# Round 0 of a top-k search reads its bank, a reversal moves to ScalarE, gates are made last, the first expert tile starts with rounded rows

## The reference

```python
probs = jax.nn.softmax(jnp.einsum('bld,de->ble', h, w_router), axis=-1)
scores = jnp.transpose(probs, (0, 2, 1))            # 16 experts x 1024 tokens
gate, idx = lax.top_k(scores, cap)                  # cap = 128
xs = jax.vmap(lambda hb, ib: hb[ib])(h, idx)
a = jnp.einsum('becd,edf->becf', xs, w_gate)        # 1024 -> 2048
u = jnp.einsum('becd,edf->becf', xs, w_up)
y = jnp.einsum('becf,efd->becd', jax.nn.silu(a) * u, w_down)
y = (y * gate[..., None]).astype(h.dtype)
out = jax.ops.segment_sum(y.reshape(-1, dm), seg, num_segments=bn * seq)
```

## Time and profile before

| | us |
|---|---|
| median of 3 runs | 2847.98 (2847.28 to 2848.88) |
| profiled execution | 2847.89 |
| its span | 2846.1 |

### The profile page before, as it was taken

How to read it: one execution, slowest core, us unless ns; L and a number is a source line. 1 busy time by engine, 2 the same in 40 slices (tenths; PEclk the granted TensorE clock), 3 DMA queues, 4 the chain that set the end, 5 groups by cost and what they waited for, 6 DMA issues and landing times.

```text
span 2846.1 us, 33534 instructions
## 1 busy us (share of the span) xinstructions
PE 2790.2 (98%) x13774; PEld 2342.7 (82%) x13774; DVE 1836.6 (65%) x2051; ACT 1514.2 (53%) x1618; POOL 136.5 (5%) x81
## 2 busy tenths in 40 slices
PE   8999999879999999999999999999999999999999
PEld 7889988768888888888888877888888888888887
DVE  8563467778888888888888895332332356544344
ACT  5322322247777777777777775333333389733022
POOL 0211000110000000000000000000000011100000
PEclk9999999989999999999999999999999999999999
DMA  6222157789999999999999951110212211243332
GB/s 200 89 77 75 71 177 263 274 310 377 388 383 390 381 389 382 381 391 382 390 384 388 380 200 74 60 53 31 60 60 60 69 48 63 95 159 132 111 133 89
DMA packets 137273, 598.97 MB, mean 210 GB/s; under 512 B 17952, under 2 KB 39840, under 8 KB 80672
## 3 DMA queue, kind: packets, MB, share of 16 engines
q1 hardware_dynamic: 132224, 580.10, 54.5%
q0 software_dynamic: 4464, 16.25, 2.2%
q10 hardware_dynamic: 432, 0.47, 0.1%
HBM read 543.06 MB, written 52.53 MB: 209 GB/s over the span
## 4 chain that ended last, share of the span: by engine, by line
PE 95%; DVE 3%; ACT 1%; issue 0%; DMA 0%; SPq 0%; DVEq 0%; ACTq 0%
PE bank L442 25%; PE bank L444 25%; PE bank L443 25%; PE bank L1835 12%; PE bank L450 3%; PE bank L2391 1%; PE bank L1406 1%; PE bank L778 1%; PE bank L2763 0%; DVE r_sc L1628 0%; DVE r_at L1629 0%; DVE r_best L1625 0%; PE bank L2392 0%; DVE b_x L2189 0%; PE bank L838 0%
## 5 line engine op out<-in xcount | busy, mean ns | idle before, releaser
L1794 DVE TENSOR_TENSOR e_wl<-e_raw,e_wh 128x2048 fp32r<-128x2048 f32 x381 | 870.8, 2292 | 126.4 <-ACT e_wh L1786 125.6
L1786 ACT ACTIVATE e_wh<-e_raw 128x2048 fp32r<-128x2048 f32 x384 | 735.8, 1919 | 187.0 <-PE bank L444 106.5
L442 PE MATMUL bank<-b_hid_h,b_wh 128*128 128x512 f32 x1152 | 454.0, 394 | 3.1 <-DVE t_v L2619 1.1
L444 PE MATMUL bank<-b_hid_h,b_wl 128*128 128x512 f32 x1152 | 449.0, 390 | 0.0
L443 PE MATMUL bank<-b_hid_l,b_wh 128*128 128x512 f32 x1152 | 448.5, 389 | 0.0
L442 PE MATMUL bank<-e_wh,e_xh 128*128 128x512 f32 x1024 | 405.7, 396 | 1.7 <-DVE e_xl L1934 1.7
L444 PE MATMUL bank<-e_wh,e_xl 128*128 128x512 f32 x1024 | 400.2, 391 | 0.0
L443 PE MATMUL bank<-e_wl,e_xh 128*128 128x512 f32 x1024 | 398.9, 390 | 0.0
L442 PEld LDWEIGHTS bank<-b_hid_h,b_wh 128*128 128x128 f32 x1152 | 216.4, 188 | 50.4 <-issue 5.4
L444 PEld LDWEIGHTS bank<-b_hid_h,b_wl 128*128 128x128 f32 x1152 | 216.2, 188 | 45.8
L443 PEld LDWEIGHTS bank<-b_hid_l,b_wh 128*128 128x128 f32 x1152 | 216.5, 188 | 42.8
(11 more groups left out here) (490 smaller groups left out, 4337.3 us busy)
## 6 DMA issues: line engine op xcount, KB each, us to landing
e_raw<-in_e_gate_dram SPq DMA_DIRECT2D x128, 1024.0 KB, 7.2
e_raw<-in_e_up_dram SPq DMA_DIRECT2D x128, 1024.0 KB, 7.7
e_raw<-in_e_down_dram SPq DMA_DIRECT2D x128, 1024.0 KB, 7.6
b_raw<-in_w_dram SPq DMA_DIRECT2D x36, 1024.0 KB, 5.8
a_raw<-in_w_dram SPq DMA_DIRECT2D x12, 1024.0 KB, 5.6
a_mod_w<-in_w_mod_dram SPq DMA_DIRECT2D x48, 256.0 KB, 4.5
a_x<-in_x_dram SPq DMA_DIRECT2D x16, 512.0 KB, 5.1
scr_sig<-a_sig SPq DMA_DIRECT2D x32, 256.0 KB, 2.3
```

Of the source, the lines that this page charges most:

```text
L442: e.matmul(out, a[0], b[0], start=first, stop=False)
L444: return e.matmul(out, a[1], b[0], start=False, stop=last)
L1786: e.activation(t.e_wh[s][:, 0:2048], t.e_raw[slot][:, 0:2048], ACT.Copy).then_inc(*e.inc("e_round", i))
L1794: e.tensor_tensor(t.e_wl[s][:, 0:2048], t.e_raw[slot][:, 0:2048], t.e_wh[s][:, 0:2048].bitcast(F32), ALU.subtract).then_inc(*e.inc("e_spli ...
```

## The change

Four edits, all around the end of the routing:

1. Round 0 of the search takes its scores from bank 4 itself; the copy to `sc[0]` is gone, and the bank is released by round 0's FIND_INDEX8.
2. The reversed values `best[:, 2]` are made by ScalarE, by an instruction at the end of `act_out` that waits for the last MAX8 (`top_found` 15). TensorE's turning of the pieces waits for it (`best_reversed`). The reversed places are made by VectorE straight from `at`, without a wait for the cast.
3. The two copies out of the bank become one, and `t.gate` is made last, behind `t.idx`; `routed` is signalled by the instruction that writes `t.idx`.
4. For tile 0, `up_products` waits for the first half of the rounded rows alone and does four matmuls high x high, four high x low, and only then waits for the first half of the low rows and does its last four.

```diff
-        self.r_pick = sb("r_pick", z + 5760, [128, 2, 16])
+        self.r_pick = sb("r_pick", z + 5760, [128, 3, 16])
...
     e.wait_ge(*e.at("best"))
+    e.wait_ge(*e.at("best_reversed"))
     e.wait_ge(*e.free(4))
...
                      ACT.Copy).then_inc(*e.evict(half, "post_taken", half))
+    e.wait_ge(*e.at("top_found", 15))
+    e.activation(t.r_best[:, 2, :], t.r_best[:, 0, ::-1], ACT.Copy).then_inc(*e.inc("best_reversed"))
...
     e.wait_ge(*e.at("scores_turned"))
-    then(e).tensor_copy(sc[0][:, :], t.bank[4][0:32, :]).then_inc(*e.evict(4))
     for r in range(16):
-        a, b = sc[r % 2], sc[1 - r % 2]
+        a, b = sc[r % 2] if r else t.bank[4][0:32, :], sc[1 - r % 2]
         top = best[:, 0, 8 * r:8 * r + 8]
...
-        e.max_index(at[:, 8 * r:8 * r + 8], top, a[:, :]).then_inc(*e.step())
+        e.max_index(at[:, 8 * r:8 * r + 8], top, a[:, :]).then_inc(*(e.step() if r else e.evict(4)))
     then(e).tensor_copy(best[:, 1, :], at[:, :]).then_inc(*e.step())
-    for i in range(2):
-        then(e).tensor_copy(best[:, 2 + i, :], best[:, i, ::-1]).then_inc(*e.step())
+    e.tensor_copy(best[:, 3, :], at[:, ::-1]).then_inc(*e.step())
     e.mark("best")
-    (ga, ia), (gb, ib) = ([t.bank[4][:, c:c + 16] for c in cs] for cs in ((0, 32), (80, 112)))
+    ga, ia = (t.bank[4][:, c:c + 16] for c in (0, 32))
+    late = t.bank[4][:, 64:128].rearrange("p (a n) -> p a n", a=2)[:, :, 16:32]
     flat = st[:, 14:16, :].rearrange("p a b -> p (a b)")
     e.wait_ge(*e.at("best_turned"))
-    then(e).tensor_copy(pick[:, 0, :], gb).then_inc(*e.step())
-    then(e).tensor_copy(pick[:, 1, :], ib).then_inc(*e.step())
-    then(e).tensor_tensor(t.gate[:, :], ga, pick[:, 0, :], ALU.max).then_inc(*e.step())
-    then(e).tensor_tensor(pick[:, 0, :], ga, pick[:, 0, :], ALU.is_ge).then_inc(*e.step())
-    then(e).tensor_tensor(flat, ia, pick[:, 1, :], ALU.subtract).then_inc(*e.step())
-    then(e).scalar_tensor_tensor(pick[:, 0, :], flat, -512.0, pick[:, 0, :], ALU.add, ALU.mult).then_inc(*e.step())
-    then(e).scalar_tensor_tensor(t.idx[:, :], pick[:, 0, :], 512.0, pick[:, 1, :], ALU.add,
-                                 ALU.add).then_inc(*e.evict(4, "routed"))
+    then(e).tensor_copy(pick[:, 0:2, :], late).then_inc(*e.step())
+    then(e).tensor_tensor(pick[:, 2, :], ga, pick[:, 0, :], ALU.is_ge).then_inc(*e.step())
+    e.tensor_tensor(flat, ia, pick[:, 1, :], ALU.subtract).then_inc(*e.step())
+    then(e).scalar_tensor_tensor(pick[:, 2, :], flat, -512.0, pick[:, 2, :], ALU.add, ALU.mult).then_inc(*e.step())
+    then(e).scalar_tensor_tensor(t.idx[:, :], pick[:, 2, :], 512.0, pick[:, 1, :], ALU.add,
+                                 ALU.add).then_inc(*e.inc("routed"))
+    e.tensor_tensor(t.gate[:, :], ga, pick[:, 0, :], ALU.max).then_inc(*e.evict(4, "gates_made"))
...
         e.wait_ge(*e.at("e_split", i))
-        e.wait_ge(*e.at("e_x", x, 1))
         if kh == 0:
             e.wait_ge(*e.free(bank))
+        if i == 0:
+            e.wait_ge(*e.at("e_x_high", x, 0))
+            for n, q in ((0, 0), (0, 1), (1, 0)):
+                if n:
+                    e.wait_ge(*e.at("e_x", x, 0))
+                for kk in range(4):
+                    m = e.matmul(t.bank[bank][:, :], t.e_x[n][:, kk, :], wt[q][:, kk, :],
+                                 start=(n, q, kk) == (0, 0, 0), stop=False)
+            m.then_inc(*e.inc("e_half", i))
+            e.mark("e_spent", i)
+            return
+        e.wait_ge(*e.at("e_x", x, 1))
         for j in range(4):
```

## The result

The changed kernel takes 2859.3 us (median of 6 runs, 2858.41 to 2863.83) against 2848.93 us for the kernel before (6 runs, 2847.28 to 2851.57): +10.4 us, a ratio of 1.0040 with a 95% interval of 1.0029 to 1.0050. Forecast were +10.4 us and 2858.3 us. The profiled execution took 2859.24 us with a span of 2857.4 us. The forecast of the time was added to 2847.98 us, the median of the three runs known then; the kernel before has 2848.93 us over six, and that is the 1.0 us between 2858.3 and 2859.3 us. The experiments are compared with further executions of the kernel before, 26 for e1 to e4 (median 2848.68 us) and 27 for e5 to e8 (2848.1 us). One of the 26 took 5716.35 us; why is not known, and the median does not rest on it.

What follows compares the result with a forecast made beforehand. TensorE, busy 98% of the span, was taken as the bound, so the first expert matmul sets the end. A delayed gather, +11.4 us, and tile 0's new start, -1.0 us, gave +10.4 us: 2858.3 us, range 2855 to 2861.5 us.

Steps and rivals of the forecast that it cites:

- The bound: TensorE busy 98% of the span; whatever moves the first expert matmul moves the end by as much.
- Part 1: Search round 0 reads the bank: nothing taken for bank reads, search ends 0.71 us earlier.
- Part 2: Reversal on ScalarE delays roundings, then GpSimd's low parts, then the gather, issued at 604.1 us: +11.4 us.
- Indices near 591 us: End of the routing on VectorE: indices ready near 591 us, ahead of the delayed gather.
- Part 3: Gates last: 0.42 us off the index work, worth nothing because GpSimd is busy until 604 us.
- Part 4: Tile 0 starts with the rounded rows: 1.41 us earlier, less a colder clock in the turning; worth -1.0 us.
- my bounds: TensorE's clock: warm 3.7 us after rows arrive gains 0.4 us; 4.4 us after first matmul costs 0.7 us.
- The sum: Whole kernel: +11.4 - 1.0 = +10.4 us on the profiled execution, forecast 2858.3 us, +0.37%.
- The dearer restart: Rival: slower GpSimd passes, matmuls cold longer, later gather landing; 2860 to 2861 us; chance 0.12.
- GpSimd is not faster once the search is over: Judges the rival that GpSimd passes alone take half, 2.25 us each: 2851.6 us; chance 0.04.
- Nothing was regained: Judges the rival that the wait is hidden or regained behind it: -2.8 us, 2845.1 us; chance 0.03.
- the likeliest case: Whole kernel, delay as priced: 2856 to 2860.5 us by GpSimd, clock and execution-spread bounds; chance 0.81.

Runs made afterwards that it cites:

- e1: The changed kernel with ScalarE's reversal put behind the three roundings instead of ahead of them; 2844.99 us against 2848.68 us, ratio 0.9989.
- e4: The kernel before with only the reversal moved to ScalarE at the end of `act_out`; 2863.46 us, ratio 1.0055.
- e5: The kernel before with only the new start of tile 0; 2846.05 us against 2848.1 us, ratio 0.9991.
- e8: e2 with VectorE's shift2 and scale2 instructions moved ahead of the index work; 2849.22 us.
- e3: The changed kernel with the gather of expert 0 behind one of GpSimd's three low-part passes instead of all; 2856.07 us over 9 runs, in two groups.
- e2: The changed kernel with GpSimd's gather of expert 0 ahead of its three low-part passes; 2856.87 us over 10 runs, in two groups.
- e7: The kernel before with only round 0 on the bank and the gates last; 2846.49 us, ratio 0.9993.
- e6: The changed kernel with the index instruction reading one of its two inputs from bank 4 instead of SBUF; 2859.19 us in one run.

## Why the prediction was right, point by point

- **The bound.** Right. What moved the first matmul moved the end, and the list of later waits is the same but for one entry.
- **Part 1.** Right, at nothing to pay: round 0, from the first MAX8 to the second, took 558.80 - 556.73 = 2.07 us on the bank. In the kernel before it took 559.75 - 557.69 = 2.06 us out of SBUF; the row that ends it, from VectorE's timeline of the kernel before:

```profile
559.75 0.66 DVE L1625 MAX8 r_best<-r_sc 32x8 f32<-32x512 f32 x1
```

The page "VectorE: DVE Perf Modes" of the Trainium skill, in its section on the TRN2 errata, would have had the round 0.19 us longer on the bank (an estimate from its figures). The two rows show 0.01 us, so for these instructions the measurement decides against the page.
- **Part 2.** Right in every step: the reversal at 588.04 us (forecast 588.3), GpSimd from 590.23 us (590.55) for 13.51 us (13.45), the gather at 603.91 us (604.1), +11.20 us where I had +11.4 us. The 0.2 us are the routing of that execution, whose scores were turned at 556.08 us and not at 556.33 us. e1 shows the cause by taking it away, e4 by doing it alone.
- **Indices near 591 us.** Wrong, 594.87 us. The step that failed is "the routing itself would have been ready near 591 us": I looked for what GpSimd's passes do to the gather, not for what they do to VectorE. It cost nothing only because the same passes also held the gather; in e3 a hold of the same instruction decided, and in e2 one of scale2.
- **Part 3.** Worth nothing in this kernel, as said. In e7 the gates-last and bank-round edits bring the gather 1.3 us forward where I had 0.71 + 0.42 = 1.1 us; of that the index work gave 0.54 us, from 592.25 - 590.99 = 1.26 us to 0.72 us.
- **Part 4.** The size was off: -1.0 us forecast, -1.44 us between the profiled executions. First matmul at 610.36 us (610.5). The clock was at 0.50 until 612.0 us and at 0.96 in the microsecond behind it, so it came back 3.6 us after the rows arrived, at the early end of my bounds. By the experiments the 1.44 us are made of three things: the new start gives 1.32 us (e5 against e7), the cold restart takes 19.43 - 18.11 = 1.32 us (the changed kernel against e5, both from turning the rows to turning hidden rows), and the profiled execution of the kernel before lost 1.44 us by its own half clock. I had set the last two against each other, 0.4 us apart. So part 4 gave something back only because the sum was made against that one execution; against one at full clock, as in e7, it would have given nothing back.
- **The sum.** +11.2 and -1.4 make +9.8 us where the experts begin; the forecast was +10.4 us. That the measured medians differ by 10.4 us too is partly chance: the profiled execution lost another 1.48 us in the second block by a half clock, which no term of the sum held, and the profiled execution of the kernel before did not have it.
- **The rivals.** The dearer restart did not occur: passes of 4.5 us, the gather landed in 4.5 us. GpSimd is not faster once the search is over: 13.51 us then, 13.45 us beside it. Nothing was regained. The bounds of the likeliest case, plainly added, give 2856.1 to 2861.7 us and not 2856 to 2860.5 us; the range of 2855 to 2861.5 us hardly changes by it.

## What to carry to other kernels

An instruction that is put on an engine "because it is idle" belongs behind the work that the engine could do before the instruction's wait ends; here two lines in the wrong place turned -3.7 us into +10.4 us. Follow the queue through every engine: what stood behind it was not ScalarE's work but a gather two queues further on. And when a delay pushes GpSimd passes over work of another engine, check that engine's two-input instructions too, since repairing the order without them (e2) left most of the loss in seven of ten executions.

## What the runs showed of the hardware

- **GpSimd's passes hold VectorE instructions with two SBUF inputs.** The same instruction of 16 columns took 0.17 us with GpSimd idle, 4.45 us beside a pass, and 0.17 us beside a pass with one input from a bank (e6). It can be held across several passes: 14.32 us in e2. The small instructions with one bank input in the same stretch took 0.16 to 0.17 us. The page "SBUF — State Buffer" of the Trainium skill, section "Who interferes with whom", says that a VectorE instruction with two SBUF inputs contends with a GpSimd instruction that reads SBUF, and that the second to start is blocked until the first ends. The holds of 3.66 to 4.45 us agree: each ended with the pass beside it, within 0.15 us if the three passes are taken as equally long. The 14.32 us of e2 do not follow from the rule as it stands. By its recorded start, 591.40 us, that instruction was 0.86 us ahead of the first pass and 0.30 us behind the start of the gather's own instruction, and it was passed over by all three passes.
- **One program can have two times here.** e2 gave 2847 us or 2857 us, e3 2852 us or 2856 us. That scale2 is held in the longer executions and not in the shorter ones is the likely reading: it took 14.32 us in e2, where one of the longer was profiled, and 0.17 us in e3, where one of the shorter was. What decides it is not shown. In both traces scale2 starts 0.30 us behind the gather and 0.86 us ahead of the next pass.
- **A half-clock stretch behind a wait of TensorE can come or not** at the same place of the same work, at 1.4 to 1.5 us each: once behind the rows' turning (kernel before 0.50, e7 1.00), once in the second block (from 1730 to 1765 us 1.00 in two profiled kernels, 0.95 in eight). For terms of 1 us this is as large as the term, and a comparison of two profiles has to look for it first.
